# Two modulation tiles per pair in 28 pairs, mLSTM outputs one step later, and the DeltaNet root taken in the mLSTM stage: one step of a DeltaNet, mLSTM and mixture-of-experts layer

## The chip, the cores and the metric

The kernel runs on one NeuronCore of a Trainium2 chip. The metric is the device time of one execution in microseconds (us). It is taken as the median of several runs; beside them stands one execution that was recorded by the hardware profiler.

## The reference, cut to what matters

One layer of a diffusion backbone works on 640 tokens (128 prompt, 512 latent) of width 2048. A conditioning vector is multiplied by `w_mod` (2048 x 12288) and gives six modulation rows (shift, scale and gate for each of two sub-layers). The token-mixing sub-layer normalises and modulates the tokens, multiplies them by `w_in`, and feeds two branches: a bidirectional gated DeltaNet (8 heads) and a bidirectional mLSTM (4 heads, value width 256). Both branch outputs are RMS-normalised per head, gated, projected and merged. Sixteen experts follow, each on its top 80 tokens.

```python
mod = (cond @ w_mod + b_mod); shift1, scale1, gate1, shift2, scale2, gate2 = split(mod, 6)
h = rmsnorm(x, pre1_gain) * (1 + scale1) + shift1
proj = h @ w_in + b_in
# mLSTM, per chunk of tokens and head
h_i = num / maximum(abs(den), exp(-m_t))          # num: chunk x 256
y_b = rmsnorm(h_f + flip(h_b), ml_onorm) * sigmoid(mo)
y_a = rmsnorm(o_dn, dn_onorm) * silu(dz)
```

## The kernel before, in words

The program is a row of stages with a barrier of all engines between them: the front (modulation and input projection), DeltaNet, mLSTM, branch outputs, merge and experts. Within a stage each engine has its own list of instructions, and semaphores tie them together. PE is TensorE, DVE VectorE, ACT ScalarE, POOL GpSimd, SP the queue that issues most loads.

**Modulation tiles.** `w_mod` comes in 96 tiles of 1 MB. PE multiplies one with `mod_products` (L398: eight short matmuls into four strips of a bank); 16 tiles make a group. When a group is complete, ACT copies its rows (`copy_mod`), PE turns them (`turn_mod`) and DVE adds the bias (`store_mod`). The first 32 tiles are done while the tokens are normalised. Four more (`EARLY_MODS = 2 * KT + 4`) are done in the classic part, before the projections with o = 21 to 24; they come through a ring of four slots in the order of `front_loads`.

**Pairs.** 29 tiles of `w_in` are projected in the classic way (`project`). The other 60 are done in 30 pairs p. A pair is one block step with seven products, in this order on PE: B11, T3, T1, T2, B21, T4, B22. One product (`part_products`, L468) is 24 matmuls of 320 columns. The parts it needs are loaded by SP (`load_part`, 512 KB each, L328) for the next pair as soon as the same product of this pair has ended; DVE forms sums of them (`t_sum`), ACT rounds them (`part_high`, L681), DVE takes the rest (`split_low`, L857). ACT and DVE also collect the products into `ob[0]` and `ob[1]`, and POOL stores these rows to DRAM (L385); in pairs 6 to 13 ACT puts a gate function on them first and POOL a gain (L383).

In pairs 0 to 19 PE also does three of the remaining 60 modulation tiles (`late_mod_chunk`), after B11, T1 and B21 (`MOD_AFTER`). They go through a single buffer `mod_slot`: SP's `load_mod` (L334) waits until the tile before has been used, then issues the next 1 MB.

```python
def late_mod_chunk(c):
    if EARLY_MODS + c < N_MOD_LOADS:
        pe.wait_ge(s["slot_in"], 16 * (c + 1))
        mod_products(EARLY_MODS + c, mod_slot)
```

After the last group DVE makes four gain and shift vectors (`VECTOR_PAIR = 21`), PE turns them in the pair behind, DVE copies them to `vec_rows` in pair 23, and POOL writes them to DRAM (`d_rows`, 64 KB) before the store of pair 24. The DeltaNet stage waits for that write.

**mLSTM.** Five steps, two directions d each. `steps` unrolls step 0 and runs the others in a loop of two bodies with register addresses. In a step DVE takes the maximum of a bank that PE filled ("Cbc", L1573), and makes `dgM` (L1582) for both directions. PE fills "Mbc" from it, ACT takes exponentials of that (`expT`, L1542), and for each d DVE then runs four operations from `carry` (L1587) to `pT` (L1592). PE's products with the state and with `pT` follow; DVE adds the numerators (L1607), updates the states (L1613), makes the reciprocal denominators `rden`, and last adds the step's outputs to `o_ml` with eight operations of 128x256 (L1637). POOL makes `diagC` (L1454) for the step ahead as soon as PE has filled "Cbc". ACT ends its step with eight squares of `o_dn` (L1558) that give `dn_ms`.

**Branch outputs.** ACT first takes the square root of the DeltaNet mean squares `dn_ms` (L1678), then 20 squares of `o_ml` (L1681), a root, two rounded copies of merge weights (L1687) and 20 scalings of `o_ml` (L1692). DVE waits for the first root, inverts it (L1720), scales `o_dn`, and gates what PE has turned.

## Time and profile before

| | us |
|---|---|
| median of 3 runs (lowest, highest) | 3562.3 (3561.23, 3562.97) |
| the profiled execution, its own time | 3563.43 |
| span of that execution, first to last instruction | 3561.6 |
| PE busy in it | 3333.4 (94%) |
| DVE busy | 2343.7 (66%) |
| ACT busy | 1777.5 (50%) |
| POOL busy | 334.1 (9%) |

The span is what the trace covers; the other 1.8 us of the profiled execution lie around it. All clock times below count from the start of the span. The classic part of the front ends near 549 us, the pairs run from there to about 1388 us, DeltaNet to 1745 us, mLSTM to 1884 us, branch outputs to 1914 us, the merge to 2419 us and the experts to the end. Matmuls are pipelined and the ends shown are modelled, so distances between matmuls are read from start to start.

### The profile page before, as it was taken

The page shows a single profiled execution, that of the slowest core. Times are in us where ns is not written, and L with a number is a line of the kernel's source. Part 1 is how long each engine was busy: PE and PEld are TensorE (multiplying, and loading weights), DVE is VectorE, ACT ScalarE, POOL GpSimd, SP SyncE. Part 2 cuts the span into 40 slices and gives each one's busy share as a digit, 9 for nine tenths or more (in the row PEclk, how much of TensorE's full clock was granted, in tenths as well). Part 3 has the DMA queues.
Part 4 walks back from the last instruction along what each step waited for, and adds up shares of the span by engine and source line. Part 5 has one row for each costly group of instructions (what it writes and reads, how often), then busy time and mean ns, then how long its engine had stood idle before and what let it go on. Part 6 is the DMA issues. An engine that isn't in the chain of part 4 may idle for free. (4 is left out here: it accounts for less than half of the span.)

```text
span 3561.6 us, 49815 instructions
## 1 busy us (share of the span) xinstructions
PE 3333.4 (94%) x19752; PEld 2733.7 (77%) x19752; DVE 2343.7 (66%) x2542; ACT 1777.5 (50%) x2276; POOL 334.1 (9%) x334
## 2 busy tenths in 40 slices
PE   5899999999999998999887999987999999999995
PEld 0899998888888998998756998874666666666663
DVE  1577556655555765455576334477888888888886
ACT  2444323323333333555545224455777777777774
POOL 0000000011100002322302100000100000010000
PEclk8999999999999999999988999998999999999997
DMA  9322325655665333121433434677999999999998
GB/s 414 148 93 93 109 96 174 209 190 198 205 209 178 114 111 106 37 53 53 126 75 138 151 117 152 231 301 270 385 383 396 396 377 397 398 374 398 396 377 320
DMA packets 181395, 796.78 MB, mean 224 GB/s; under 512 B 17508, under 2 KB 75108, under 8 KB 102004
## 3 DMA queue, kind: packets, MB, share of 16 engines
q1 hardware_dynamic: 163204, 702.37, 53.4%
q0 software_dynamic: 17168, 86.98, 7.3%
q10 hardware_dynamic: 864, 5.27, 0.4%
q8 instruction: 104, 1.70, 0.2%
q14 instruction: 55, 0.45, 0.0%
HBM read 732.10 MB, written 62.46 MB: 223 GB/s over the span
## 5 line engine op out<-in xcount | busy, mean ns | idle before, releaser
L2502 DVE TENSOR_TENSOR expert_lo<-expert_ring,first_expert_hi 128x2048 fp32r<-128x2048 f32 x288 | 660.0, 2292 | 111.8 <-ACT first_expert_hi L2439 108.0
L2439 ACT ACTIVATE first_expert_hi<-expert_ring 128x2048 fp32r<-128x2048 f32 x285 | 546.8, 1918 | 175.1 <-PE bank L2386 175.1
L2385 PE MATMUL bank<-expert_lo,xeT_hi 128*80 128x512 f32 x1024 | 402.0, 393 | 0.0
L468 PE MATMUL bank<-h_hi,part_hi 128*128 128x320 f32 x960 | 300.3, 313 | 6.7 <-DVE part_lo_b L857 3.7
L2384 PE MATMUL bank<-first_expert_hi,xeT_hi 128*80 128x512 f32 x768 | 303.3, 395 | 1.3 <-DVE xeT_lo L2507 1.3
L2386 PE MATMUL bank<-first_expert_hi,xeT_lo 128*80 128x512 f32 x768 | 299.5, 390 | 0.0
L468 PE MATMUL bank<-h_lo,part_hi 128*128 128x320 f32 x960 | 297.6, 310 | 0.0
L681 ACT ACTIVATE part_hi<-part_x 128x1024 fp32r<-128x1024 f32 x120 | 127.4, 1061 | 246.4 <-PE bank L468 227.6
L857 DVE TENSOR_TENSOR part_lo_x<-part_x,part_hi 128x1024 fp32r<-128x1024 f32 x120 | 149.3, 1244 | 150.9 <-ACT part_hi L681 143.4
L2502 DVE TENSOR_TENSOR expert_lo<-expert_ring,expert_hi 128x2048 fp32r<-128x2048 f32 x96 | 219.6, 2287 | 43.6 <-ACT expert_hi L2439 43.5
L468 PE MATMUL bank<-s_hi,part_hi 128*128 128x320 f32 x720 | 227.9, 317 | 1.7 <-DVE part_lo_x L857 1.7
L468 PE MATMUL bank<-s_lo,part_hi 128*128 128x320 f32 x720 | 223.4, 310 | 0.0
L433 PE MATMUL bank<-h_hi,win_hi 128*128 128x320 f32 x928 | 214.9, 313 | 4.7 <-DVE win_lo L766 3.0
L2439 ACT ACTIVATE expert_hi<-expert_ring 128x2048 fp32r<-128x2048 f32 x96 | 183.7, 1913 | 70.7 <-PE bank L2386 53.3
L2385 PEld LDWEIGHTS bank<-expert_lo,xeT_hi 128*80 128x80 f32 x1024 | 151.5, 148 | 81.1 <-issue 0.5
L433 PE MATMUL bank<-h_lo,win_hi 128*128 128x320 f32 x928 | 211.7, 309 | 0.0
L433 PE MATMUL bank<-h_hi,win_lo 128*128 128x320 f32 x928 | 211.6, 309 | 0.0
L681 ACT ACTIVATE part_hi<-part_b 128x1024 fp32r<-128x1024 f32 x90 | 95.3, 1061 | 227.7 <-PE bank L468 227.6
L2385 PE MATMUL bank<-expert_lo,hiddenT_hi 128*80 128x512 f32 x512 | 200.8, 392 | 0.0
L468 PEld LDWEIGHTS bank<-h_hi,part_hi 128*128 128x128 f32 x960 | 181.4, 189 | 24.6 <-issue 23.7
L468 PEld LDWEIGHTS bank<-h_lo,part_hi 128*128 128x128 f32 x960 | 181.4, 189 | 0.0
L433 PEld LDWEIGHTS bank<-h_hi,win_hi 128*128 128x128 f32 x928 | 154.4, 188 | 13.8 <-issue 6.0
(406 smaller groups left out, 7814.3 us busy)
## 6 DMA issues: line engine op xcount, KB each, us to landing
expert_ring<-d_wgate SPq DMA_DIRECT2D x128, 1024.0 KB, 7.1
expert_ring<-d_wup_e SPq DMA_DIRECT2D x128, 1024.0 KB, 7.8
expert_ring<-d_wdown SPq DMA_DIRECT2D x128, 1024.0 KB, 10.4
mod_slot<-d_wmod SPq DMA_DIRECT2D x60, 1024.0 KB, 7.3
part_b<-d_win SPq DMA_DIRECT2D x90, 512.0 KB, 3.7
front_ring<-d_wmod SPq DMA_DIRECT2D x36, 1024.0 KB, 8.2
front_ring<-d_win SPq DMA_DIRECT2D x29, 1024.0 KB, 4.9
d_proj<-out_rows POOLq DMA_DIRECT2D x86, 320.0 KB, 2.4
```

Of the source, the lines that this page charges most:

```text
L433: mm = pe.matmul(bank[b][c][:, 0:HALF_T], wt[:, kk, :], h[:, c, kk, :], start=(kk == 0 and wt is hi and h is k.h_hi), stop=(kk == KT - 1 a ...
L468: mm = pe.matmul(part_bank[j][:, 0:HALF_T], w, a[:, kk, :], start=(kk == 0 and x == 0), stop=(kk == HALF_K - 1 and x == 2))
L681: act.activation(part_hi[m % HI_SLOTS][:], part(p, j)[:], ACT.Copy).then_inc(s["part_high"], 1)
L857: dve.tensor_tensor(part_lo(*divmod(m, 7))[:], part(*divmod(m, 7))[:], full(part_hi[m % HI_SLOTS][:]), ALU.subtract).then_inc(s["part_low" ...
L2384: pe.matmul(out[0:CAP, :], a_hi, hi, start=first, stop=False)
L2385: pe.matmul(out[0:CAP, :], a_hi, lo, start=False, stop=False)
L2386: return pe.matmul(out[0:CAP, :], a_lo, hi, start=False, stop=last)
L2439: act.activation(w_hi[n % NSPLIT][:], w[:, n % NSLOT].rearrange("p (k n) -> p k n", n=HALF), ACT.Copy).then_inc(s["we_high"], 1)
L2502: dve.tensor_tensor(w_lo[n % NSPLIT][:], w[:, n % NSLOT].rearrange("p (k n) -> p k n", n=HALF), w_hi[n % NSPLIT][:].bitcast(F32), ALU.subt ...
```

## The change

`EARLY_MODS` grows by four, so eight tiles instead of four are done in the classic part, before the projections with o = 17 to 24, and their loads stand in the ring ahead of the loads of o = 19 to 26. The pairs do the remaining 56 with two per pair in pairs 0 to 27, after B11 and after T2. The group ends move from pairs 3, 9, 14 and 19 to 3, 11, 19 and 27; the vectors from pair 21 to 28. Their rows are copied by DVE in pair 29, after the sum that follows B21, and written to DRAM by SP, which waits for the write before it issues the last two stores of the front.

In the mLSTM stage DVE's steps are unrolled with constant addresses, and the outputs of a step are added in the next step, behind `dgM`; those of the last step stand at the end. ACT takes the root of `dn_ms` at the end of this stage, and DVE inverts it there.

```diff
-EARLY_MODS = 2 * KT + 4
+EARLY_MODS = 2 * KT + 8
...
-MOD_AFTER = (B11, T1, B21)
-VECTOR_PAIR = 21
+MOD_AFTER = (B11, T2)
+VECTOR_PAIR = 28
...
-        if 23 <= o < 27:
-            loads.append(("mod", 2 * KT + o - 23))
+        if 19 <= o < 27:
+            loads.append(("mod", 2 * KT + o - 19))
...
-                    for j, sem in ((B11, "b11_in"), (T3, "b12_in"), (T1, "b22_in"), (B21, "b21_in")):
-                        if p + 1 < N_PAIRS:
+                    for j, sem in ((B11, "b11_in"), (T3, "b12_in"), (T1, "b22_in"), (T2, None), (B21, "b21_in")):
+                        if p + 1 < N_PAIRS and sem:
...
-                            load_mod(3 * p + 1 + MOD_AFTER.index(j))
+                            load_mod(2 * p + 1 + MOD_AFTER.index(j))
+                sp.wait_ge(s["vec_copied"], 1)
+                sp.dma_start(k.d_rows.rearrange("v (k p) -> (v k) p", p=P), vec_rows).then_inc(k.rows_out, 16)
+                sp.wait_ge(k.rows_out, 16)
                 for b in range(2):
                     sp.wait_ge(s["out_made"], MADE * N_PAIRS - 1 + b)
...
-                    if p == VECTOR_PAIR + 3 and n % 2 == 0:
-                        pool.wait_ge(s["vec_copied"], 1)
-                        pool.dma_start(k.d_rows.rearrange("v (k p) -> (v k) p", p=P), vec_rows).then_inc(k.rows_out, 16)
...
-                    if 21 <= o < 25:
-                        mod_chunk(2 * KT + o - 21)
+                    if 17 <= o < 25:
+                        mod_chunk(2 * KT + o - 17)
...
                     part_products(p, B11)
-                    late_mod_chunk(3 * p)
+                    late_mod_chunk(2 * p)
...
                     part_products(p, T1)
-                    late_mod_chunk(3 * p + 1)
                     part_products(p, T2)
+                    late_mod_chunk(2 * p + 1)
...
                     part_products(p, B21)
-                    late_mod_chunk(3 * p + 2)
...
-                    if p == VECTOR_PAIR + 2:
-                        dve.wait_ge(s["vec_turned"], 1)
-                        dve.tensor_copy(vec_rows, k.bank[4][:, 0:P]).then_inc(s["vec_copied"], 1)
                     dve.wait_ge(s["part_summed"], part_number(p, B21) + 1)
...
                     made.then_inc(s["out_made"], 1)
+                    if p == VECTOR_PAIR + 1:
+                        dve.wait_ge(s["vec_turned"], 1)
+                        dve.tensor_copy(vec_rows, k.bank[4][:, 0:P]).then_inc(s["vec_copied"], 1)
...
                 steps(act, body)
+                act.drain()
+                act.activation(k.dn_rs[:], k.dn_ms[:], ACT.Sqrt, bias=k.eps, scale=1.0 / P).then_inc(dn_rooted, 1)
...
+                places = [(step, (TT - step) % TT) for step in range(TT)]
+                def outputs(step):
+                    if step == 0:
+                        dve.wait_ge(o_zeroed, 1)
+                    for d in range(2):
+                        for h in range(4):
+                            o = col(k.o_ml[:], places[step][d], h * DV_ML, (h + 1) * DV_ML)
+                            dve.scalar_tensor_tensor(out=o, in0=nu[d][:, h, 0:DV_ML], scalar=rden[d][:, h:h + 1],
+                                                     in1=o, op0=ALU.mult, op1=ALU.add)
+                        dve.drain()
...
                         dve.tensor_tensor(dgM[d][:], all_heads(k.ident), per_head(nM[d][:], P), ALU.mult
                                           ).then_inc(s[d]["dgM"], 1)
+                    if step > 0:
+                        outputs(step - 1)
...
-                    if x == 0:
-                        dve.wait_ge(o_zeroed, 1)
-                    for d in range(2):
-                        for h in range(4):
...
-                steps(dve, body)
+                for step in range(TT):
+                    body(step, places[step], min(step, 1))
+                outputs(TT - 1)
+                dve.wait_ge(dn_rooted, 1)
+                dve.reciprocal(k.dn_rs[:], k.dn_rs[:])
...
             def _(act):
-                act.activation(dn_rs[:], k.dn_ms[:], ACT.Sqrt, bias=k.eps, scale=1.0 / P).then_inc(dn_rooted, 1)
...
-                dve.wait_ge(dn_rooted, 1)
-                dve.reciprocal(dn_rs[:], dn_rs[:])
-                dve.drain()
                 scale_dn(0)
```

## Rows read from the trace of the kernel before

**Rows 1.** Two stretches: length, busy PE, PEld, DVE, ACT, POOL, granted clock, DMA, GB/s

```profile
554.78:1115.27 560.49, 542.34 (x3664) 479.86 (x3661) 339.24 (x361) 176.99 (x207) 47.81 (x54) 0.99 0.59 201
...
1756.23:1884.20 127.97, 104.62 (x485) 78.80 (x483) 97.02 (x300) 61.83 (x237) 9.15 (x8) 0.91 0.46 119
```

**Rows 2.** Waits of PE and of DVE: total us, times, longest us

```profile
PE bank L398 <- DMA mod_slot<-d_wmod: 13.7, 26, 1.3
...
DVE part_x L831 <- issue: 5.8, 29, 0.5
```

**Rows 3.** The tile mod_slot: from the issue of its 60 loads to landing

```profile
DMA to landing us min/median/max: 5.2/7.3/8.6
```

**Rows 4.** PE around one modulation tile, which lies between these two matmuls

```profile
782.25 0.31 PE L468 MATMUL bank<-h_hi,part_lo_b 128*128 128x320 f32 x1
...
783.71 0.31 PE L468 MATMUL bank<-h_lo,part_hi 128*128 128x320 f32 x1
```

**Rows 5.** SP's issues: after B11 of pairs 1, 7, 8, 19; after B21 of 20, 21

```profile
587.88 0.33 SPq L328 DMA_DIRECT2D part_b<-d_win  x1
...
760.42 0.33 SPq L328 DMA_DIRECT2D part_b<-d_win  x1
...
794.32 0.33 SPq L328 DMA_DIRECT2D part_b<-d_win  x1
...
1115.27 0.33 SPq L328 DMA_DIRECT2D part_b<-d_win  x1
...
1158.64 14.41 SPq L328 DMA_DIRECT2D part_b<-d_win  x3
...
1183.28 0.33 SPq L328 DMA_DIRECT2D part_b<-d_win  x1
```

**Rows 6.** ACT and POOL in pair 7

```profile
768.92 0.53 ACT L710 ACTIVATE out_rows<-bank,chan 128x320 f32<-128x320 f32 x1 [8.06 <-DMA d_proj<-out_rows]
...
761.34 0.58 POOL L385 DMA_DIRECT2D d_proj<-out_rows  x1 [3.87 <-issue]
```

**Rows 7.** DMA issues: count, KB each, median us to landing

```profile
d_rows<-mod_rows POOLq DMA_DIRECT2D x1, 64.0 KB, 2.2
```

**Rows 8.** DVE in the mLSTM stage, in order of time

```profile
1756.23 0.69 DVE L1573 TENSOR_REDUCE maxC<-bank 128x4 f32<-128x512 f32 x1 [2.53 <-PE bank L1479]
...
1760.40 0.69 DVE L1582 TENSOR_TENSOR diagM<-const,negM 128x512 f32<-128x512 f32 x1
...
1781.94 0.69 DVE L1573 TENSOR_REDUCE maxC<-bank 128x4 f32<-128x512 f32 x1 [0.27 <-issue]
...
1808.78 0.69 DVE L1573 TENSOR_REDUCE maxC<-bank 128x4 f32<-128x512 f32 x1 [0.16 <-issue]
...
1812.43 0.69 DVE L1582 TENSOR_TENSOR diagM<-const,negM 128x512 f32<-128x512 f32 x1
...
1816.86 0.16 DVE L1587 TENSOR_TENSOR carry<-ms,negMend 128x4 f32<-128x4 f32 x1 [1.99 <-ACTq L1544]
...
1817.39 0.68 DVE L1592 SCALAR_TENSOR_TENSOR pT<-bank,expT 128x512 f32<-128x512 f32 x1
...
1829.60 2.46 DVE L1637 SCALAR_TENSOR_TENSOR o_ml<-numerator,rden,o_ml 128x256 f32 x4 [0.17 <-issue]
...
1859.88 0.69 DVE L1573 TENSOR_REDUCE maxC<-bank 128x4 f32<-128x512 f32 x1 [0.16 <-issue]
...
1882.53 1.67 DVE L1637 SCALAR_TENSOR_TENSOR o_ml<-numerator,rden,o_ml 128x256 f32 x4 [0.17 <-issue]
```

**Rows 9.** POOL while DVE adds the outputs of step 2

```profile
1830.08 1.30 POOL L1454 TENSOR_TENSOR diagC<-const,ci 128x512 f32<-128x512 f32 x1 [22.93 <-PE bank L1479]
```

**Rows 10.** ACT in the branch outputs

```profile
1886.59 1.28 ACT L1678 ACT_TABLE_LOAD   x1 [9.06 <-PEq L2579]
...
1888.12 0.40 ACT L1681 ACTIVATE y_parts<-o_ml 128x256 f32<-128x256 f32 x1
...
1900.10 8.09 ACT L1692 ACTIVATE o_ml<-o_ml,ml_rs 128x256 f32<-128x256 f32 x20
```

More of the change, by code:

```diff
@@ L1391, in phase_mlstm @@
         state_in, state_out, prompt_done = k.sem("ml_state_in"), k.sem("ml_state_out"), k.sem("ml_prompt_done")
-        o_zeroed, gates_in = k.sem("ml_o_zeroed"), k.sem("bo_gates_in")
+        o_zeroed, gates_in, dn_rooted = k.sem("ml_o_zeroed"), k.sem("bo_gates_in"), k.sem("dn_rooted")
         square = sb("dn_square", [P, H_DN, P])
@@ L1567, in _, with body @@
                 dve.drain()
-                def body(step, tiles, x, buf, loads):
+                places = [(step, (TT - step) % TT) for step in range(TT)]
[8 more added lines that the diff above has]
+                        dve.drain()
+                def body(step, tiles, x):
                     for d in range(2):
@@ L1631, in body @@
                     dve.drain()
-                    if x == 0:
-                        dve.wait_ge(o_zeroed, 1)
-                    for d in range(2):
-                        for h in range(4):
-                            o = col(k.o_ml[:], tiles[d], h * DV_ML, (h + 1) * DV_ML)
-                            dve.scalar_tensor_tensor(out=o, in0=nu[d][:, h, 0:DV_ML], scalar=rden[d][:, h:h + 1],
-                                                     in1=o, op0=ALU.mult, op1=ALU.add)
-                        dve.drain()
-                steps(dve, body)
+                for step in range(TT):
[3 more added lines that the diff above has]
+                dve.reciprocal(k.dn_rs[:], k.dn_rs[:])
 def phase_branch_outputs(nc, k):
@@ L1652, in phase_branch_outputs @@
         ml_ms = sb("ml_ms", [P, TT, H_ML])
-        dn_rs, ml_rs = sb("dn_rs", [P, TT, H_DN]), sb("ml_rs", [P, TT, H_ML])
-        dn_rooted, ml_rooted, ml_rs_made, dn_scaled, ml_scaled, turned, read = (k.sem("bo_" + n) for n in (
-            "dn_rooted", "ml_rooted", "ml_rs_made", "dn_scaled", "ml_scaled", "turned", "read"))
+        ml_rs = sb("ml_rs", [P, TT, H_ML])
+        ml_rooted, ml_rs_made, dn_scaled, ml_scaled, turned, read = (k.sem("bo_" + n) for n in (
+            "ml_rooted", "ml_rs_made", "dn_scaled", "ml_scaled", "turned", "read"))
         BANKS = 8
@@ L1698, in scale_dn @@
                     v = k.o_dn[:, t, :].rearrange("p (h n) -> p h n", n=P)
-                    dve.tensor_tensor(v, v, per_head(dn_rs[:, t, :], P), ALU.mult).then_inc(dn_scaled, 1)
+                    dve.tensor_tensor(v, v, per_head(k.dn_rs[:, t, :], P), ALU.mult).then_inc(dn_scaled, 1)
                 def gate(b, t):
@@ L1717, in gate @@
                         op.then_inc(read, 1)
-                dve.wait_ge(dn_rooted, 1)
-                dve.reciprocal(dn_rs[:], dn_rs[:])
-                dve.drain()
                 scale_dn(0)
@@ L2622, in build @@
             k.z_gate, k.mo_gate = (sb(front, n, [P, 8, T]) for n in ("z_gate", "mo_gate"))
-            k.dn_ms = sb(front, "dn_ms", [P, TT, H_DN])
+            k.dn_ms, k.dn_rs = (sb(front, n, [P, TT, H_DN]) for n in ("dn_ms", "dn_rs"))
             phase_mlstm(nc, k)
```

## The prediction

> **What bounds the kernel now.** I read the table of busy time by stretch first. In the pairs that carry modulation tiles PE is busy 542 of 560 us at a granted clock of 0.99; in the mLSTM stage DVE works 97 of 128 us and PE's clock is 0.91 of its 2.4 GHz [rows 1]. So a microsecond counts in the pairs where PE stands still, and in mLSTM where the chain through DVE is cut. Then the waits: PE's wait for `mod_slot` comes 26 times, up to 1.3 us [rows 2]. Then SP's queue, whose issue after B11 marks each pair: a pair without tiles takes 1183.28 - 1158.64 = 24.64 us, while pairs 1 to 6 take 172.54 / 6 = 28.76 and pairs 8 to 18 take 320.95 / 11 = 29.18 [rows 5]. A pair has 168 matmuls, so one takes 0.147 us, and a tile costs PE (783.71 - 782.25) - 2 x 0.147 = 1.17 us when it is there in time [rows 4]. Three tiles should make 24.64 + 3.51 = 28.15. The rest is waiting: 17 x 28.15 = 478.6 against 493.5 measured, 15 us.
>
> **Tiles in the pairs.** Between two tiles lie two products (7.04 us), then two, then three. A load is issued when the tile before has been used, and lands 5.2 to 8.6 us later, 7.3 in the median [rows 3]: two products don't cover that. After the change the gaps are three products (T3, T1, T2, 10.6 us) and four (14.1 us). Even the slowest load, 8.6, is covered, so the waits go: **-15 us**. In SP's queue the tile's load still stands behind B11's part; the load after T2 makes SP wait for the tile behind T2, and queued behind that wait is only the part for B21, which can't be issued before B21 ends. Pairs 20 to 27 get two loads of 1 MB each that they didn't have; their parts then come beside tiles as in pairs 0 to 19, where three such loads a pair left PE no other waits than the two named next. A pair with two tiles should take 24.64 + 2.34 = 27.0 us. The group ends (copy, turn, bias) move with the tiles and keep their number and their place inside the pair.
>
> Pair 7 took 794.32 - 760.42 = 33.9 us [rows 5]. Here ACT waited 8.06 us for a store that POOL had issued late [rows 6], and T2 waited for ACT's rounding. That chain starts in pair 6 and doesn't touch the tiles, so T2 starts no earlier; the tile that stood after T1 was hidden in this wait. Hence 59 tiles were paid for, and 56 will be: -3 x 1.17 = **-3.5 us**. Pair 0 has a wait for the sums of its first step; I take it unchanged.
>
> **Tiles in the classic part.** Four more at 1.17 us: **+4.7 us**. PE has no gap there that could hide them. Their loads share the ring with the weights; the same alternation already stood at o = 23 to 26, and each weight tile still has more than one projection as lead.
>
> **Vectors.** Making them in pair 28 instead of 21 costs DVE the same short operations beside PE's products; nothing waits there, as in pair 21. The copy in pair 29 waits for a turn that PE has done before B21. The 64 KB write leaves POOL's queue, where it stood ahead of a store, and enters SP's, ahead of the last two stores. It takes 2.2 us [rows 7], while T4 and B22 take 7.0, and the last store waits for B22: 0 us; if that cover went, 2.2.
>
> **mLSTM.** After `dgM` of the second direction DVE is idle until ACT has its exponentials: 1.99 us before the second `carry` [rows 8]. The eight output operations now run there. In the old place they collide with POOL's `diagC`, which takes 1.30 us [rows 9]: four take 2.46 us beside it and 1.67 without [rows 8]. Step 0 shows the new collision, since no outputs stand ahead of it: its head (`maxC` to the second `dgM`) takes 1760.40 + 0.69 - 1756.23 = 4.86 us, that of step 2 takes 4.34. A step after the change is then: head 4.86, outputs 2 x (1.67 + 0.17) = 3.7, two blocks from `carry` to `pT` of 1817.39 + 0.68 - 1816.86 = 1.2 each, 2.4 together, then the tail from `pT` to `rden`, 1829.60 - 0.17 - 1818.07 = 11.4, and 0.4 until PE has the next "Cbc" (an estimate; 0 to 1). Sum 22.8. ACT's second release came 3.7 us after `dgM`, the second block needs it after 3.7 + 1.2 = 4.9, so ACT isn't late.
>
> Before, steps 1 to 3 took 1859.88 - 1781.94 = 77.9 us: 3 x 22.8 = 68.4, -9.5. Step 0 loses its outputs at the end, about 2 x 2.46 + 0.17 = 5.1, and gains the 0.4: -4.7. Step 4 took 1882.53 + 1.67 - 1859.88 = 24.3; it becomes 4.34 + 3.7 + 2.4 + 11.4 + 3.7 and some 0.4 for the reciprocal, 25.9: +1.6. Together **-12.6 us**. At the low end only the visible idle time counts, 4 x 1.99 less the 1.6, some 6 us; at the high end POOL's collisions vanish altogether and the register gaps of 0.2 go too, 16. I take the chain, since each of its pieces has a row.
>
> **Branch outputs.** The stage's end hangs on ACT's scaling of `o_ml`, behind 20 squares, a root and two copies, from 1900.10 us on [rows 10]; DVE's last gates wait for it. Table load and root delay the squares by 1888.12 - 1886.59 = 1.5 us [rows 10]; both go to the end of mLSTM, where ACT has ended its squares long before DVE. **-1.5 us**; 0 if the merge weights, loaded at the stage's start, are late.
>
> The Trainium skill, "ScalarE: Activation LUTs", section What ACT_TABLE_LOAD costs, puts a switch of tables at 1283 ns and a drain of about 1380 ns. The load of 1.28 us agrees, but the trace has no such drain behind it; by the page's 2.7 us this term would be about -2.7.
>
> **Sum.** -15 - 3.5 + 4.7 - 12.6 - 1.5 = -27.9 us. The profiled execution took 3563.4 (its span 3561.6), the median is 1.1 lower: 3535.5 or 3534.4. I forecast **3535 us**. The merge and the experts only shift.
>
> **Rivals.** *The loads stay late.* With two tiles in each of 28 pairs the parts and tiles may land later than 10.6 us. For it speaks that PE waited longest in pairs 8 to 18, where loads and stores meet; against it, the 8.6 maximum. If half of each wait stays the gain falls by 7, if all of it by 15: 3542 to 3550. Chance 0.07.
>
> *mLSTM isn't DVE's chain.* If PE's or ACT's part of the step simply takes up what DVE frees, the stage gains 4 us: 3544. For it: DVE waits for PE and ACT inside the tail, too. Against: the outputs stand on the only path to the next `maxC`, whose wait there is 0.16 to 0.27 us of issue [rows 8]. Chance 0.12.
>
> *Unrolled code is fetched late.* DVE's loop of two bodies becomes straight code. The longest unexplained stop of DVE in the straight code of the pairs is 0.5 us, the longest of any engine that I read is POOL's 3.87 [rows 2, 6]; two stops of that size give 3543. Chance 0.04. The Trainium skill, "Advanced Engine Details and Errata", section ISA Cache, speaks against unrolling: two cache lines of 256 instructions per engine. That the front's straight code on DVE runs with stops of 0.5 us at most is all that the trace has on it.
>
> *Slower than before.* In the pairs the slot's load would have to land later than 10.6 us after its issue in all 28 pairs. Each further microsecond costs 28; from 10.6 + 28 / 28, about 11.6, the gain is eaten, and at 12.2 us, two thirds above the median of 7.3, the time is 3535 + 45 = 3580. Chance 0.02.
>
> *It doesn't do what it says*, because the waits that PE loses return as waits for ACT's rounding and DVE's chain is held by ACT: 3559, within the measurement. Chance 0.02.
>
> **How the numbers follow.** The forecast has 0.73. Its own range: the mLSTM ends (6 to 16) and the table drain give 3530 to 3542; the clock in mLSTM and the slow spells behind waits in pairs 0 and 7 may give or take another 4. The range 3526 to 3549 takes in the first three rivals too. What a measurement of this kernel can tell from no change is about 0.2%, 7 us. Faster by more than that: 0.73 + 0.07 + 0.12 + 0.04, less 0.01 for their tails, 0.95; within it 0.03; slower 0.02.
>
> **What would show it.** PE's wait for `mod_slot` gone from its list, pairs 8 to 18 at 27.0 us, pairs 20 to 27 too; 56 loads of `mod_slot`. The classic part ends 4.7 us later, the pairs about 14 us earlier. In mLSTM `maxC` to `maxC` 22 to 23 us, no idle time ahead of the first `carry`, the outputs without a POOL operation beside them. ACT's squares of `o_ml` at the start of the branch stage. It is wrong if new waits of PE for parts appear in pairs 20 to 27, if the steps of mLSTM stay above 25 us, or if the pairs' saving is under 8 us.

## The result and the profile after

The changed kernel takes 3541.56 us (median of 4 runs, 3538.98 to 3542.67) beside 3562.64 us for the kernel before on the same chip (3561.23 to 3565.14): ratio 0.9942, 95% interval 0.993 to 0.9955. The forecast was 3535 in a range of 3526 to 3549. The gain is 21.1 us where 27.9 were forecast. The profiled execution took 3542.4 us, its span is 3540.6 us against 3561.6.

The busy table by stretch, of the changed kernel: the pairs from their first product to DeltaNet's first, then mLSTM from the first `maxC` to the last output [rows 1]. Columns as there.

```profile
558.28:1386.77 828.49, 813.31 (x5505) 753.39 (x5505) 524.52 (x574) 271.39 (x315) 64.42 (x78) 0.99 0.50 170
1748.18:1865.70 117.52, 100.24 (x485) 78.28 (x483) 93.36 (x300) 63.69 (x239) 8.33 (x8) 0.94 0.49 129
```

In the kernel before, the same two stretches take 845.21 and 127.96 us. Next PE's waits, changed kernel (us in total, times, longest), and the landing of `mod_slot`:

```profile
PE bank L1506 <- DVE pT L1607: 11.8, 6, 2.8
...
PE bank L468 <- DVE part_lo_x L856: 8.2, 2, 4.5
...
PE bank L468 <- DVE part_lo_b L856: 3.7, 1, 3.7
...
issue: 10.8, 56
...
DMA to landing us min/median/max: 4.6/6.9/8.7
```

PE's wait for `mod_slot` [rows 2] is gone: the only idle time ahead of the 56 tiles is 10.8 us on the side that loads PE's weights, 0.19 us a tile. The landing times are nearly those of before [rows 3]; what changed is that at least 10.6 us lie between issue and use. At the top stands a wait that had no such weight before: PE for `pT`, 11.8 us in 6 waits, 3.5 in 5 before. SP's issues behind B21 in pairs 1, 2, 7, 19 and 27 (x2 or x3: the issue behind B11 of the next pair, and one more in the last row, are merged into the row of B21):

```profile
614.04 10.89 SPq L328 DMA_DIRECT2D part_b<-d_win  x2
...
641.01 10.89 SPq L328 DMA_DIRECT2D part_b<-d_win  x2
...
782.81 10.89 SPq L328 DMA_DIRECT2D part_b<-d_win  x2
...
1106.82 10.89 SPq L328 DMA_DIRECT2D part_b<-d_win  x2
...
1322.96 14.41 SPq L328 DMA_DIRECT2D part_b<-d_win  x3
```

A pair takes 641.01 - 614.04 = 26.97 us where three tiles took 28.76 to 29.18 [rows 5], and from B21 of pair 7 to B21 of pair 27 it is (1322.96 - 782.81) / 20 = 27.0 us a pair. DVE in mLSTM, in order of time, two steps:

```profile
1791.17 0.69 DVE L1586 TENSOR_REDUCE maxC<-bank 128x4 f32<-128x512 f32 x1 [0.48 <-PE bank L1478]
...
1795.69 0.68 DVE L1595 TENSOR_TENSOR diagM<-const,negM 128x512 f32<-128x512 f32 x1
1796.30 3.41 DVE L1578 SCALAR_TENSOR_TENSOR o_ml<-numerator,rden,o_ml 128x256 f32<-128x256 f32 x8
1799.78 0.16 DVE L1602 TENSOR_TENSOR carry<-ms,negMend 128x4 f32<-128x4 f32 x1
...
1801.24 0.68 DVE L1607 SCALAR_TENSOR_TENSOR pT<-bank,expT 128x512 f32<-128x512 f32 x1
...
1814.58 0.24 DVE L1645 RECIPROCAL rden<-rden 128x4 f32<-128x4 f32 x2
...
1815.30 0.69 DVE L1586 TENSOR_REDUCE maxC<-bank 128x4 f32<-128x512 f32 x1 [0.48 <-PE bank L1478]
```

The outputs stand in what was idle time and take 3.41 us for eight, with no POOL operation beside them [rows 8, 9]. But the tail, from the end of `pT` (1801.92) to the end of `rden` (1814.82), takes 12.90 us where 11.4 had been read. The branch outputs, ACT:

```profile
1859.27 1.28 ACT L1561 ACT_TABLE_LOAD   x1
1860.57 0.33 ACT L1561 ACTIVATE dn_rs<-dn_ms,chan 128x40 f32<-128x40 f32 x1
1867.87 0.42 ACT L1692 ACTIVATE y_parts<-o_ml 128x256 f32<-128x256 f32 x1 [6.98 <-PEq L2587]
```

Table load and root now lie ahead of the stage [rows 10]; the root starts 0.02 us behind the load. From the last output to the merge's first product it is 29.94 us, before 31.63.

By stage, from the two traces (us; the last column is the sum that the prediction made):

| stretch | before | after | difference | forecast |
|---|---|---|---|---|
| start to the pairs' first product | 549.45 | 558.28 | +8.8 | +4.7 |
| pairs, to DeltaNet's first product | 845.21 | 828.49 | -16.7 | -18.5 |
| DeltaNet, to the first `maxC` | 361.58 | 361.41 | -0.2 | 0 |
| mLSTM, to the last output | 127.96 | 117.52 | -10.4 | -12.6 |
| branch outputs, to the merge | 31.63 | 29.94 | -1.7 | -1.5 |
| merge and experts | 1645.80 | 1644.98 | -0.8 | 0 |

Three rows differ from the forecast by over a microsecond: the start by 4.1, the pairs by 1.8, mLSTM by 2.2. The experiments go after the first and the last.

### The profile page after: what moved, and what is told of

The parts are those of the page before. It is cut to its first block and busy times, and to the rows that moved or that the text cites. A ratio compares the mean times of both kernels' runs of the same rounds, so it can differ in the third digit from the quotient of the medians.

```text
span 3540.6 us, 49727 instructions
## 1 busy us (share of the span) xinstructions
PE 3332.9 (94%) x19752; PEld 2737.8 (77%) x19752; DVE 2341.5 (66%) x2542; ACT 1778.2 (50%) x2276; POOL 332.9 (9%) x333
## 6 DMA issues: line engine op xcount, KB each, us to landing
expert_ring<-d_wdown SPq DMA_DIRECT2D x128, 1024.0 KB, 10.4
```

## Experiments

The tables behind each group are read from the traces as above: one profiled execution of each kernel. "Before" in a group are runs of the kernel before on the same chip; all together they scatter over 12 us (3553.8 to 3566.1), those of the changed kernel over 3 to 4.

### Each part alone, and the change once more

Edit of `tiles_alone`: the constants, loads, queue rows and vectors of the diff; mLSTM and branch outputs as before. `outputs_alone`: DVE's part of mLSTM, without the root:

```diff
+                    if step > 0:
+                        outputs(step - 1)
...
-                steps(dve, body)
+                for step in range(TT):
+                    body(step, places[step], min(step, 1))
+                outputs(TT - 1)
```

`root_alone`, with DVE's loop as before:

```diff
                 steps(act, body)
+                act.drain()
+                act.activation(k.dn_rs[:], k.dn_ms[:], ACT.Sqrt, bias=k.eps, scale=1.0 / P).then_inc(dn_rooted, 1)
...
                 steps(dve, body)
+                dve.wait_ge(dn_rooted, 1)
+                dve.reciprocal(k.dn_rs[:], k.dn_rs[:])
...
```

`changed_again` is the changed kernel, unedited.

> Only the tiles, the vectors and the queue rows of the change; mLSTM and branch outputs as before. Theory: the waits for mod_slot (15 us) go, the pairs gain 17 to 18 us, the classic part pays 4.7, so the kernel gains 12 to 14 us (3549 to 3551) and pairs with two tiles take 27.0 us. In the trace of the changed kernel DeltaNet started only 7.9 us earlier; rival: the 2.6 us lost ahead of 130 us and the 1.5 us behind the wait at 524 us belong to the change, then they are here again and the gain is 8 to 9 us (3554).

> Only the mLSTM outputs a step later (with DVE's steps written out); tiles and root as before. Theory: the stage gains 10 us as in the changed kernel (3552 to 3554), steps of 20.8, 22.2, 24, 24, and the stretch from the end of pT to the end of rden is 12.9 us in steps 2 to 4 where 11.4 was forecast, with PE's first products behind pT at half clock. Rival: the 12.9 came from what the tiles and the root changed (the loads, ACT's end), then the stretch is 11.4 here and the stage gains 12.6 (3550).

> Only the root of the DeltaNet squares in the mLSTM stage; tiles and outputs as before. Theory: table load and root (1.5 us) and DVE's wait for them leave the front of the branch outputs, gain 1.5 to 2.2 us (3560.5 to 3561). Rival: ACT's squares wait for something else, gain under 0.5 us.

> The changed kernel a second time. Theory: the 2.6 us lost ahead of 130 us and the slow spell behind the wait at 524 us vary from run to run, so at least one of them is smaller here and DeltaNet starts at 1380 to 1386 us; the time is 3539 to 3543 us. Rival: both are there as before (DeltaNet at 1387), then they belong to the change. The steps of mLSTM are the same to 0.3 us in both traces by either.

| kernel | time, us | ratio to before, interval |
|---|---|---|
| `tiles_alone` | 3551.86 (3547.39 to 3554.05) | 0.9976 (0.9965 to 0.9986) |
| `outputs_alone` | 3547.77 (3544.90 to 3551.45) | 0.9963 (0.9951 to 0.9976) |
| `root_alone` | 3558.94 (3553.70 to 3567.99) | 1.0001 (0.9991 to 1.0010) |
| `changed_again` | 3541.19 (3539.45 to 3542.15) | 0.9945 (0.9932 to 0.9958) |

The first two ratios and the last agree with a sum: 0.24% + 0.37% = 0.61%, against 0.55% for the whole. Neither part met its expected time: `tiles_alone` lies between theory (3549 to 3551) and rival (3554), `outputs_alone` below both (3552 to 3554, 3550). The root can't be told from nothing in these times; in its trace the stretch from last output to merge is 30.35 us instead of 31.63, so 1.3 us are there and the scatter of the kernel before covers them.

`outputs_alone` has mLSTM at 117.49 us and tails of 11.41, 11.36, 12.90, 12.89 and 13.02: the long tail comes with this part. The rival that tiles or root cause it is out; that the loop written out doesn't cause it either is shown by `steps_unrolled` below, whose tails stay at 11.4.

In `tiles_alone` the pairs take 828.47 us and the gain of the waits is there, but DeltaNet starts at 1386.25, as its rival said; `changed_again` has it at 1386.73. By the letter of the expectations the 4.1 us at the start belong to the tiles. With more traces, most of them don't (*When the first product starts*, below).

### The gap between the two tiles

```diff
-MOD_AFTER = (B11, T2)
+MOD_AFTER = (B11, T1)
...
                     part_products(p, T1)
+                    late_mod_chunk(2 * p + 1)
                     part_products(p, T2)
-                    late_mod_chunk(2 * p + 1)
```

> The changed kernel with the second tile of a pair ahead of T2 instead of behind it, so that between the two tiles lie two products (T3, T1: 7.0 us) and then five. Theory (the three-product gap covers a load of up to 8.7 us, two products don't): PE's wait for mod_slot is back in some 15 to 28 pairs at 0.3 to 1 us each, and the time is 3547 to 3558. Rival (the loads were late because three of them came in a pair; two come sooner): PE waits for mod_slot under 2 us in all, and the time stays at 3540 to 3543.

It took 3554.48 us (3547.17 to 3558.26; ratio 0.9976, 0.9967 to 0.9986), by the medians 13 and by the ratios 11 us more than `changed_again`, and scatters over 11 us again. The profiled execution is the shortest of its nine runs. PE's waits and the landing in it:

```profile
PE bank L398 <- DMA mod_slot<-d_wmod: 9.3, 14, 1.7
...
DMA to landing us min/median/max: 5.2/7.3/8.8
```

The pairs take 838.28 us, 9.8 more than in the changed kernel. This wait is 9.3 us. The two aren't the same microseconds: pair 7 is 3.6 us shorter here (29.88 instead of 33.53), so the other pairs lose 13.4, some 4 of them to something else. The number of tiles and of loads is the changed kernel's; only one gap went from three products to two. So the gap decides, not the number of loads in a pair. The scatter goes with it: over all runs, kernels of this study with a gap of two products scatter over 7 to 14 us, those with three over 2 to 7. That loads which land between 5 and 9 us after their issue make this scatter is likely, since 7.0 us don't cover them and 10.6 do, but it isn't shown: one execution of each kernel was traced.

### The clock behind PE's wait for pT

PE around `pT` of step 4 in the changed kernel (L1502: products of the old state, L1506: of `pT`; start, us for the group):

```profile
1845.17 0.60 PE L1502 MATMUL bank<-Cs,ml_staged 128*128 128x257 f32 x2
1848.20 0.70 PE L1506 MATMUL bank<-ml_vtok,pT 128*128 128x257 f32 x2 [2.43 <-DVE pT L1607]
1848.73 0.60 PE L1502 MATMUL bank<-Cs,ml_staged 128*128 128x257 f32 x2
1849.22 1.21 PE L1506 MATMUL bank<-ml_vtok,pT 128*128 128x257 f32 x2
1850.22 1.07 PE L1502 MATMUL bank<-Cs,ml_staged 128*128 128x257 f32 x2
1851.08 1.06 PE L1506 MATMUL bank<-ml_vtok,pT 128*128 128x257 f32 x2
1851.93 0.97 PE L1502 MATMUL bank<-Cs,ml_staged 128*128 128x257 f32 x2
1852.74 0.60 PE L1506 MATMUL bank<-ml_vtok,pT 128*128 128x257 f32 x2
```

PE stands 2.43 us, and soon after, four groups take 0.97 to 1.21 us instead of 0.60: the granted clock from 1849.3 to 1852.6 us is 0.50, that is 1.2 instead of 2.4 GHz. DVE, which adds each of these products to a numerator, is held up with them. In the kernel before, the first `pT` ended 1.7 to 2.8 us behind `diagM`; it is 4.5 now. That kernel had half-clock spells in this stage, too, but behind another stand: PE waited 14.1 us for `diagM`, in 7 waits, and the clock was at 0.50 mostly ahead of the second `pT`, as from 1812.8 to 1816.1 us in step 2. Only in step 1 did such a spell reach 1.0 us into the tail, to 1792.2, and that tail took 11.83 us instead of 11.4.

`kept_busy` gives PE something to do in that wait: the QK products twice over (the second set overwrites the first with the same values), made behind the products of `diagM`:

```diff
-                        mm.then_inc(b["A"].filled, 1)
                     for d in range(2):
...
+                    for d in range(2):
+                        b = bank[d]
+                        for h in range(8):
+                            mm = pe.matmul(b["A"].t[:, h % 4 * P:(h % 4 + 1) * P], staged[d][:, 4 + h % 4, :], staged[d][:, h % 4, :],
+                                           start=True, stop=True)
+                        mm.then_inc(b["A"].filled, 1)
```

`products_ahead` fills the wait with work that has to be done anyway: the four products of the old state for heads 0 and 1 go ahead of the first product of `pT`. `old_state` holds the lines that made such a product in the loop below.

```diff
+                    def old_state(h, d):
...
+                    for h in range(2):
+                        for d in range(2):
+                            old_state(h, d)
                     for h in range(4):
                         for d in range(2):
...
+                            if h > 1:
+                                old_state(h, d)
...
```

> The changed kernel with the QK products of mLSTM made twice, and only behind the products of dgM: PE works some 2 us of its wait for pT on products that are thrown away, and nothing else moves. Theory (the 1.5 us by which the tail missed the forecast are PE's clock at 1.2 GHz behind the wait): no half-clock products behind pT in steps 2 to 4, the tail is back at 11.4 to 11.9 us there, and the kernel takes 3536 to 3538.5. Rival (the tail is longer for another reason, such as the order in which DVE meets ACT's and PE's results): the tail stays at 12.9 and the time at 3540 to 3543 or above.

> The changed kernel with PE's four products of the old state for heads 0 and 1 (0.43 us each) put ahead of the first product of pT, into the wait for pT that has grown to 2.4 to 2.8 us. Theory (the tail from pT to rden is paced by PE, and longer than forecast since PE's clock falls in that wait): the tail shrinks from 12.9 to 10 to 11.4 us in steps 2 to 4, steps take 21 to 22.5 us, and the kernel takes 3528 to 3536. Rival (ACT or DVE pace the tail): steps as before within 0.5 us, 3539 to 3542.

`kept_busy`, step 4, the same groups and DVE's last operations of `pT` and `rden`:

```profile
1843.50 3.73 PE L1494 MATMUL bank<-ml_staged 128*128 128x128 f32 x32
1847.07 0.60 PE L1507 MATMUL bank<-Cs,ml_staged 128*128 128x257 f32 x2
1847.51 0.60 PE L1511 MATMUL bank<-ml_vtok,pT 128*128 128x257 f32 x2
1847.94 0.60 PE L1507 MATMUL bank<-Cs,ml_staged 128*128 128x257 f32 x2
1848.37 0.60 PE L1511 MATMUL bank<-ml_vtok,pT 128*128 128x257 f32 x2
```

```profile
1847.27 0.69 DVE L1612 SCALAR_TENSOR_TENSOR pT<-bank,expT 128x512 f32<-128x512 f32 x1 [0.39 <-PE bank L1494]
1859.34 0.24 DVE L1650 RECIPROCAL rden<-rden 128x4 f32<-128x4 f32 x2
```

Every group is at 0.60, and the tail is 1859.58 - 1847.96 = 11.62 us; so are those of all other steps (11.61 to 11.67). So 1.3 of the 1.5 us go once PE doesn't stand; the forecast tail of 11.4 holds to 0.3. Steps 2 and 3 go from 24.13 and 23.76 to 22.90 and 22.67 us. Steps 0 and 1, which had no long tail, pay 1.9 and 0.5 us for the extra products, so the stage as a whole gains 0.9 (116.6) and the kernel takes 3539.88 us (3536.85 to 3542.41; 0.9934, 0.9921 to 0.9948), a little above the 3536 to 3538.5 that were expected and not to be told from the changed kernel's. What shows the cause is the trace.

`products_ahead` took 3533.21 us (3532.42 to 3537.36; 0.9919, 0.9905 to 0.9932): tails of 10.92, 10.80, 12.18, 10.81 and 10.80, stage 111.4 us, 6.1 less than the changed kernel's. In the changed kernel the tail is paced by PE, not by ACT or DVE. In step 2 the clock still falls, now behind the first `pT`.

### When the first product starts

`start_shifted` moves the loads of the two constants:

```diff
-                sp.dma_start(k.chan[:], k.d_chan).then_inc(s["chan_in"], 16)
-                sp.dma_start(k.const[:], k.d_const).then_inc(s["const_in"], 16)
                 for place, (kind, n) in enumerate(FRONT_LOADS):
                     slot = place % FRONT_SLOTS
+                    if place == 4:
+                        sp.dma_start(k.chan[:], k.d_chan).then_inc(s["chan_in"], 16)
+                        sp.dma_start(k.const[:], k.d_const).then_inc(s["const_in"], 16)
```

> The changed kernel with SP's two loads of the constants issued behind the first four tiles, so that the first products start up to 0.9 us earlier; nothing else moves. The three traces with the tiles of the change show the granted clock at 0.66 to 0.70 at 115 to 120 us and 0.67 to 0.74 at 525 to 530, the three without show 1.00. Theory (the clock's fall there hangs on when the first products start, 0.3 us later with the change): one of the two spells is gone or shorter, DeltaNet starts 1 to 4 us earlier than 1386.8, and the kernel takes 3537 to 3540. Rival (the clock's fall comes from the tiles themselves): both spells stay, and the time is 3540 to 3543.

The first product came 10.8 us later than in the changed kernel instead of up to 0.9 earlier (26.56 us), so the edit missed its aim; it moved the start all the same. The granted clock is 1.00 at 115 to 120 and at 525 to 530 us, and DeltaNet starts at 1385.54. The time, 3544.95 us (3541.01 to 3545.78; 0.9949, 0.9936 to 0.9963), is above both expectations; the profiled execution is the shortest of the five, and what the others lost isn't in it.

All kernels of this study side by side then tell more than the single run:

| kernel | first product | clock 115 to 120 | clock 525 to 530 | pairs start | pairs last | span |
|---|---|---|---|---|---|---|
| before | 15.52 | 1.00 | 1.00 | 549.45 | 845.2 | 3561.6 |
| `root_alone` | 15.51 | 1.00 | 1.00 | 549.31 | 841.3 | 3554.8 |
| `outputs_alone` | 15.60 | 1.00 | 1.00 | 549.48 | 847.2 | 3549.7 |
| `steps_unrolled` | 15.70 | 1.00 | 1.00 | 549.44 | 844.6 | 3556.4 |
| changed | 15.77 | 0.66 | 0.67 | 558.28 | 828.5 | 3540.6 |
| `changed_again` | 15.85 | 0.66 | 0.70 | 558.18 | 828.5 | 3540.2 |
| `tiles_alone` | 15.85 | 0.70 | 0.74 | 557.78 | 828.5 | 3550.1 |
| `ahead_and_split` | 15.75 | 0.66 | 0.68 | 558.29 | 828.7 | 3536.9 |
| `gap_of_two` | 15.56 | 1.00 | 0.86 | 555.89 | 838.3 | 3545.3 |
| `kept_busy` | 15.51 | 1.00 | 0.86 | 555.77 | 829.6 | 3538.3 |
| `root_undone` | 15.57 | 1.00 | 0.89 | 555.62 | 829.0 | 3540.0 |
| `products_ahead` | 15.64 | 1.00 | 0.94 | 555.45 | 828.9 | 3531.4 |
| `ahead_in_pairs` | 15.50 | 1.00 | 0.96 | 555.38 | 828.8 | 3530.8 |

Every kernel from the fifth row on has the tiles of the change, and ahead of the pairs all nine are the same program. Five of them, whose first product came at 15.50 to 15.64, have the full clock at 115 us; the four at 15.75 to 15.85 have not. In those four the pairs start at 557.8 to 558.3, in the five at 555.4 to 555.9. So some 2.6 us of the 4.1 go with a start that is 0.2 us later, not with the tiles. Product by product, the changed kernel lies 0.2 us behind `root_undone` at 99 us, 1.1 at 102 us and 2.7 from 120 us on: the clock parts the two kinds already at 99.8 to 100.8 us (0.50 in the four, 1.00 in the others). That the start is the cause is not shown: the one run that was to set it came far later and had the full clock. Nor is it known whether the tiles make the late kind more frequent; none of the four kernels without them has it.

The remaining 1.5 us are in all nine. There a wait of 3 us for DVE's `win_lo`, which every kernel has and which ends at 517.27 in the kernel before, ends 4 to 7 us later, and in the 4 us behind it the granted clock is 0.57 to 0.62 and not 1.00: 17 or 18 matmuls start in them, and 27 in the kernel before. (In the column from 525 to 530 a kernel whose wait ends at 522 shows only the end of this spell, hence its 0.86 to 0.96.) `start_shifted` has all the tiles and 1.00 behind this wait, too, so the tiles alone don't bring the fall; what does stays open. The rows of the two kinds, changed kernel first, then `root_undone`, then the wait's end in the kernel before (columns as in the busy table):

```profile
115.00:120.00 5.00, 5.00 (x26) 4.96 (x27) 1.95 (x3) 2.55 (x5) 1.93 (x3) 0.66 0.01 3
524.58:528.58 4.00, 4.00 (x17) 4.00 (x18) 4.00 (x2) 2.42 (x2) 0.00 (x0) 0.57 0.56 198
```

```profile
115.00:120.00 5.00, 5.00 (x40) 4.76 (x38) 2.73 (x4) 3.42 (x7) 2.51 (x4) 1.00 0.00 0
521.91:525.91 4.00, 4.00 (x17) 4.00 (x18) 4.00 (x2) 2.42 (x2) 0.00 (x0) 0.59 0.56 196
```

```profile
517.27:521.27 4.00, 4.00 (x27) 4.00 (x28) 4.00 (x2) 2.44 (x2) 0.00 (x0) 1.00 0.58 202
```

In the first stretch PE is busy all 5 us in both, yet it starts 26 matmuls in one kernel and 40 in the other: busy time alone doesn't show a half clock.

### The root undone, the steps written out, and the wait for pT split

`root_undone` is the changed kernel with the root and DVE's reciprocal back in the branch outputs. `steps_unrolled` is the kernel before with DVE's loop written out and the outputs at the end of their own step, as they were:

```diff
...
-                steps(dve, body)
...
+                    outputs(step)
...
+                for step in range(TT):
+                    body(step, places[step], min(step, 1))
```

`ahead_and_split` is `products_ahead` with the outputs of each direction right ahead of its own block:

```diff
-                    if step > 0:
-                        outputs(step - 1)
                     for d in range(2):
+                        if step > 0:
+                            outputs(step - 1, (d,))
                         b = bank[d]
```

and `ahead_in_pairs` gives that kernel another order of heads and directions on PE, ACT and DVE:

```diff
+        heads = [(h0 + j, d) for h0 in (0, 2) for d in range(2) for j in range(2)]
...
-                    for h in range(4):
-                        for d in range(2):
+                    for h, d in heads:
```

> The changed kernel with the root of the DeltaNet squares back in the branch outputs, where the tiles keep the runs close together. Theory: the stretch from the last output of mLSTM to the first product of the merge is 31.0 us as in the kernel with the outputs alone, 1.1 us longer than the 29.9 of the changed kernel, and the kernel takes 3541.5 to 3543.5. Rival (the merge waits for its weights instead): the stretch is 29.9 and the time 3539.5 to 3541.5.

> The kernel before with DVE's five mLSTM steps written out, but the outputs at the end of their own step. Theory (straight code costs DVE nothing; the gain is the outputs' place): steps of 25.7, 26 to 27, 26 to 27 and 24 to 25 us as before, the stage within 1 us of 128.0, and the kernel at 3558 to 3563. Rival (code is fetched late): steps longer by 0.5 us or more, with DVE waiting for issue above 1 us. Second rival (the loop itself cost DVE its jump): steps 0.5 us shorter or more, stage 125.5 to 127.

> The kernel with the products ahead, and with the four outputs of each direction right ahead of that direction's block, so that pT of the first direction ends about 2.8 us behind dgM and not 4.5, and that of the second at 5.5 as before. Theory (PE's clock in the tail hangs on how long PE stands ahead of the first pT): the half-clock spell of step 2 (tail 12.2) goes, the tails are 10.4 to 10.8, and the kernel takes 3530 to 3533. Rival (the wait moves to the second pT and is as long): the tails stay at 10.8 and one of 12.2, the time at 3533 to 3537.

> As the last, and PE, ACT and DVE take heads 0 and 1 of the first direction, then of the second, then heads 2 and 3 likewise, so that PE has two products to do between the two pT. Theory (PE paces the tail by its order): the first products are out when DVE comes to the numerators, the tails are 9.8 to 10.5 us, and the kernel takes 3526 to 3531. Rival (DVE paces the tail by now: products of kw, eight numerators, eight states, 0.42 to 0.69 us each): tails as in the last kernel within 0.2 us and the time within 1 us of it.

| kernel | time, us | ratio to before, interval | tails of the five steps | stage |
|---|---|---|---|---|
| before | 3562.64 (3561.23 to 3565.14) | 1 | 11.42, 11.83, 11.35, 11.36, 11.35 | 128.0 |
| changed | 3541.56 | 0.9942 (0.9930 to 0.9955) | 11.42, 11.36, 12.90, 12.90, 13.05 | 117.5 |
| `root_undone` | 3542.26 (3539.84 to 3543.70) | 0.9951 (0.9939 to 0.9964) | 11.41, 11.36, 12.89, 12.90, 13.04 | 117.5 |
| `steps_unrolled` | 3555.72 (3550.73 to 3558.37) | 0.9986 (0.9977 to 0.9995) | 11.42, 11.37, 11.36, 11.36, 11.37 | 123.8 |
| `ahead_and_split` | 3536.95 (3535.31 to 3538.74) | 0.9936 (0.9924 to 0.9948) | 10.91, 10.79, 12.18, 12.18, 10.79 | 113.2 |
| `ahead_in_pairs` | 3532.93 (3532.20 to 3533.95) | 0.9926 (0.9914 to 0.9938) | 10.91, 10.78, 10.78, 10.79, 10.78 | 110.4 |

The root: from the last output to the merge it is 31.03 us without the move, 29.94 with it, 1.1 us beside the late outputs, as the theory said. The other 0.6 us to the 31.63 of the kernel before come with the straight code: `steps_unrolled` has 31.01. The time is 1.1 us above `changed_again`, inside both scatters: the trace shows it, the times are only in line with it.

The loop: writing it out makes the stage 4.2 us shorter than in the trace of before, and 2 to 3 shorter than in `tiles_alone` and `root_alone`, which have the loop (125.8, 127.1). I had expected nothing; the second rival had the sign, not the size. DVE's stretch from `rden` to the next `maxC` is 5.13 us in steps 1 and 2 instead of 5.70 and 5.85. In the loop DVE stands again and again where nothing but its own issue is seen:

```profile
DVE o_ml L1637 <- issue: 1.8, 8, 0.5
```

With `ms` (1.6) and `maxC` (1.2) that makes 4.6 us in the stage of the kernel before, and the same in `tiles_alone` and `root_alone`; in `steps_unrolled` it is 0.6. So of the stage's 10.4 us, 2 to 4 come from the straight code, and some 6 from the place of the outputs (123.8 to 117.5).

The split: it brings the first `pT` from 4.5 to 2.8 us behind `diagM`, but with heads and directions in the old order PE does one product and waits for the second `pT`; two tails stay at 12.18. The rival holds there. With two heads of one direction after the other PE has more to do in between, and no tail is long any more. DVE and PE in step 4 of `ahead_in_pairs`:

```profile
1838.37 0.68 DVE L1614 SCALAR_TENSOR_TENSOR pT<-bank,expT 128x512 f32<-128x512 f32 x1
1838.97 1.66 DVE L1585 SCALAR_TENSOR_TENSOR o_ml<-numerator,rden,o_ml 128x256 f32<-128x256 f32 x4
1841.13 0.68 DVE L1614 SCALAR_TENSOR_TENSOR pT<-bank,expT 128x512 f32<-128x512 f32 x1
...
1852.36 0.24 DVE L1652 RECIPROCAL rden<-rden 128x4 f32<-128x4 f32 x2
```

```profile
1837.49 1.90 PE L1500 MATMUL bank<-Cs,ml_staged 128*128 128x257 f32 x8
1839.22 1.03 PE L1513 MATMUL bank<-ml_vtok,pT 128*128 128x257 f32 x4
1841.87 1.14 PE L1513 MATMUL bank<-ml_vtok,pT 128*128 128x257 f32 x4 [1.62 <-DVE pT L1614]
1842.84 0.59 PE L1500 MATMUL bank<-Cs,ml_staged 128*128 128x257 f32 x2
```

The wait is down to 1.62 us and nothing behind it runs at half clock. But the tails were to be 9.8 to 10.5, and are 10.8 with either order: in that of step 4 DVE is busy 9.0 of 10.8 us and waits 1.3 for ACT's numerators. Its own work and this wait pace it by now. The time is above the expected 3526 to 3531, and against `products_ahead` (3533.21) there is no gain that the times can tell. Both versions beat the changed kernel by some 8 us.

## Why the prediction was right, and where it was off

*Waits for the tiles, -15 us, and three tiles fewer, -3.5.* Right in kind, 1.8 short of the size. Pairs with two tiles take 26.97 us (27.0 forecast), the last eight too; no wait for `mod_slot` is left; `gap_of_two` shows that the three-product gap does it. The step that missed is that pair 0's wait was taken unchanged: it is a wait for DVE's sums and roundings, and PE with a tile less just gets to it sooner. The pair was to get 1.17 us shorter and got 0.9 longer (35.63 us, 34.72 before). Its row is

```profile
587.99 0.61 PE L468 MATMUL bank<-h_hi,part_hi 128*128 128x320 f32 x1 [4.48 <-DVE part_lo_x L856]
```

and from this product to the one ahead it is 4.8 us, 3.3 before: taking a tile out of this pair saved nothing, as the prediction had seen for pair 7, and the products behind run at half clock (0.47 us each where 0.31 is the rule) for some 5 us, 3.3 before. ACT's wait for a late store in pair 7 stayed [rows 6]:

```profile
768.04 0.53 ACT L709 ACTIVATE out_rows<-bank,chan 128x320 f32<-128x320 f32 x1 [7.75 <-DMA d_proj<-out_rows]
```

The chain isn't fixed: in `gap_of_two` the pair took 29.88 us instead of 33.53. What shortened it isn't shown.

*Classic part, +4.7.* The four tiles cost that, 4.67 us in the trace. The sum had no term for the clock ahead of and behind them: 4.1 us in the profiled execution, of which 2.6 go with the start and 1.5 with the wait that ends at 524.58 us. The prediction looked at the granted clock for mLSTM and pairs 0 and 7 only ("another 4" in its range); the 1.5 would have been looked for by asking it of each wait of some microseconds whose place moves. The 2.6 differ between executions of the same code ahead of the pairs, so nothing in the one trace of before could have given them.

*Vectors, 0.* Their write is SP's now, 64 KB landing in 1.7 us, and pair 29, in which they are turned, takes 24.91 us, as pair 22 did before.

*mLSTM, -12.6.* Measured -10.4, and the figure holds two causes of which the sum named one (register gaps stood only in the high end). It put 0.4 us in the place of all that stood from `rden` to the next `maxC`, and so gave the outputs' place credit for what the loop took; `steps_unrolled` shows that 2 to 4 us are the straight code's. Step 0 lost 4.9 (4.7 forecast). Steps 1 to 3 took 22.21, 24.13 and 23.76 where 22.8 was forecast for each, the last 26.6 instead of 25.9. The head is 4.83 us in steps 1 and 3 and 5.21 in step 2, `rden` to `maxC` 0.48, outputs with the two blocks 5.5 instead of 6.1: within 0.4 of the forecast or better. The mis-sized term is the tail: 11.4 was read where PE had its first `pT` early; in steps 2 to 4 it is 12.9 to 13.05, since PE's longer wait is followed by a half clock. `kept_busy` shows this as the cause of 1.3 of the 1.5 us. That step 1 has the same 4.5 us between `diagM` and `pT` and a tail of 11.36 says that the fall is no fixed consequence of the wait's length. The busy table from `pT` on, steps 1 and 4 of the changed kernel:

```profile
1776.00:1788.00 12.00, 9.64 (x44) 8.23 (x45) 9.77 (x29) 7.92 (x36) 0.00 (x0) 1.00 0.34 89
...
1846.00:1859.00 13.00, 10.80 (x41) 9.01 (x42) 9.25 (x27) 7.81 (x35) 0.00 (x0) 0.87 0.00 0
```

The granted clock is 1.00 in the one and 0.87 in the other. Why the one step keeps it stays open.

*Branch outputs, -1.5.* Measured -1.7, in part by luck: the root brought 1.1 to 1.3 (`root_undone`, `root_alone`), the straight code 0.6 that no term had. The Trainium skill, "ScalarE: Activation LUTs", section What ACT_TABLE_LOAD costs, adds a drain of about 1380 ns to the load; with it the term would have been 2.7. The rows don't show one: the load starts 0.06 us behind the operation ahead of it, and the root 0.02 us behind the load's end.

*The rivals.* The loads are not late. The DVE chain does set mLSTM's step, but what sits in it, PE's products behind `pT`, became slower: part of the second rival came true. The third did not: straight code made the stage shorter, not longer. The Trainium skill, "Advanced Engine Details and Errata", section ISA Cache, gives an engine two cache lines of 256 instructions. That this speaks against unrolling was the prediction's own conclusion; `steps_unrolled` shows a gain where that would have been a loss.

The sum: -27.9, +4.1 for the clock at the start, +1.8 for pair 0 and its slow products, +2.2 for the tails, -0.2 for the branch, -1.0 for DeltaNet and the merge, makes -21.0. That is the difference of the two spans.

## What to carry to other kernels

A prefetch with one buffer is a race between its landing time and the work between two uses: compare the gap with the slowest landing in the trace, not with the median, and spread the uses evenly rather than in equal numbers. Work moved into an engine's idle time lengthens the wait of whoever comes next; ask of that engine not only how long it stands but at what clock it goes on, and put work that is ready (here the products of the old state) into that wait. Where a kernel's runs scatter, look for a transfer that is covered only just: here the kernels with cover to spare scattered less (2 to 7 us against 7 to 14), though no run shows that this is why.

## What the runs showed of the hardware

The granted clock at 115 us went with a difference of 0.2 us in the start of the first product, 100 us earlier: 1.00 in the nine kernels of the table whose first product came by 15.70, 0.66 to 0.70 in the four that came from 15.75 on. Two traces of the same kernel had it alike, and three kernels alone against three others looked like an effect of the change. What sets it stays open. A granted clock is best compared over all traces at hand before it is put down to an edit, and in windows that start at the same event, not at the same time.

DVE's five steps written out instead of looped took 2 to 4 us off a stage of 128, without any operation moved; the idle time ahead of DVE's operations that only its own issue ends went from 4.6 to 0.6 us.
